# A decoder step: casts moved from GpSimd to ScalarE, a candidate key moved from PSUM to SBUF, and one wait of TensorE placed earlier

## The chip, the cores and the metric

The kernel runs on one core of a Trainium2 chip. The metric is the device time of one execution in microseconds (us). The engines are named as in the profile: PE is TensorE, DVE is VectorE, ACT is ScalarE, POOL is GpSimd, SP is SyncE, whose queue issues the transfers; PEq, ACTq, DVEq, POOLq and SPq are their sequencers. A line number such as L1545 is one of the kernel before.

## The reference

One layer of a hybrid decoder for 1024 prompt tokens and 8 decoding tokens, all in float32, model width 1024.

```python
h = modulate(rms_norm(x, ln1_g), sh1, sc1)          # sh, sc, g from silu(c) @ ada_w + ada_b
xr, gr, q, k, v, iq, ik, iw = split(h @ w_in)
xc, conv_new = causal_conv(xr, ...)                  # width 4
hr = rg_lru(xc, ...);  out_a = gelu(gr) * hr         # group A: linear recurrence
q, k = rope(rms_norm(q)), rope(rms_norm(k))          # group B: sparse attention
score = sum_h iw[h] * relu(iq[h] . ik)               # causal
idx = top_k(score, 256)                              # per query
out_b = softmax(q . k[idx]) @ v[idx]
x = x + g1 * (concat(rms_norm(out_a), rms_norm(out_b)) @ w_out)
x = x + g2 * ((silu(h2 @ w_gate) * (h2 @ w_up)) @ w_down)   # h2 from x as h above
```

## The kernel before

**Precision.** Each float32 product is made of three matmuls. An operand is split into a high part (a cast to fp32r, tiles `wH`, `cH`, `hH`) and a low part (what the cast left out, `wL`, `cL`, `hL`), and high times high, high times low and low times high are added up in PSUM. For every weight tile there is therefore a load (`wraw` or `craw`), a cast for the high part and a subtraction for the low part. The subtractions (`low`, `chunk_low`) run on POOL, the casts (`high`, `chunk_high`) mostly on ACT.

**The stage around the change** runs from about 137 to 304 us. Four things go on at once, tied by semaphores and by the order in which each engine's instructions are written.

1. *The threshold search.* For each query the 256th largest score is found by setting the bits of an integer key one after another, in `KEY_BITS` = 32 rounds. The queries are in seven groups (`NSEL`) with rows of 384 to 1025 scores. In round r, DVE counts the scores of four groups that are at least the candidate key (L1486), ACT does the other three (`signs(r)`, L973). DVE then compares the counts with a limit (L1526, L1543) and copies, under the mask `keep`, the raised candidate over the lowered one (L1545), which gives the next candidate `keyX`; both are made at the start of a round by `candidates` (L1499, an exclusive-or with a bit of `flips`). `limit`, `flips` and `raised` lie in PSUM bank 7; keys, mask and counts lie in SBUF. The copy raises `s_thr`, on which ACT's next `signs` waits.
2. *The rest of the projection.* PE computes q, k and v for nine token tiles from three weight chunks, 27 products (`NQKV`), each evacuated by ACT (`qkv_evac`) in the round that `qkv_bit` gives, 1 + n*16//26: the last in round 17. The weights of the chunk with number 3 (128x2048) are loaded when chunk 1 is used up; PE needs its low part `cL` for the last nine products.
3. *The units of the recurrent group.* Eight units of 128 weight columns (`unit`, L2238 to L2240), each 72 matmuls over all tokens, evacuated by `unit_evac` in the rounds of `UNIT_BIT`. Behind each unit PE makes the columns of the ada modulation (L2227) and the next ada product (L2221) from `adb`, a single buffer that SP loads again for each. DVE brings a row of each product to SBUF (`ada_row_late`), in fixed places of its program: behind the rounds 21, 23, 26, 28 and 31 of the search and then in the stage that follows it. Units 3 to 7 have their high parts cast by ACT in the rounds of the unit three before; the units 0 to 2 are loaded early, and POOL casts them and subtracts, once `s_thr` is at 1.
4. *POOL's row.* Behind units 0 to 2, POOL squares, scales by the gain and rotates the heads in three phases (`squared`, `rotated`, `scaled`), of which the roots are taken on DVE and ACT in rounds 8 to 10, 14 to 16 and 20 to 22. Between phase 0's rotation and its scaling stands chunk 3: a cast (L793) and the subtraction (L679). Behind phase 2's rotation come the four convolutions, with the low parts of units 3 to 7 between them. SP can issue the load of a unit and of `adb` only in the order written, behind the `wL` that frees the slot.

When the search is over, DVE turns the keys into thresholds, settles ties, and builds gates (up to about 378 us); attention, the output projection and the FFN follow. They wait for that stage.

PE asks for 24 evacuations ahead of unit 0, and for all 27 behind it:

```python
                pe.wait_ge(s_pqe, 24 if u == 0 else NQKV)
```

Of the kernel before, what the change touches and what calls it, by code (L numbers as in the profile page):

```python
# [8 lines left out]
ALU = mybir.AluOpType  # L9
# [5 lines left out]
I32 = mybir.dt.int32  # L15
# [11 lines left out]
ALLT = NTT + 1  # L27
# [32 lines left out]
NQKV = 3 * ALLT  # L60
# [14 lines left out]
SLOTS = 3  # L75
# [10 lines left out]
NSEL = len(SEL)  # L86
SEL_ACT = 4
KEY_BITS = 32

def score_banks(i, g):  # L90
    return (2 + g % 2, 3 + g % 2) if i < 4 else (2 * (g % 2), 2 * (g % 2) + 2)
# [55 lines left out]
def unit_bit(u):  # L147

    return UNIT_BIT[u]


def high_bit(u):

    return unit_bit(u - SLOTS)


def halves(w):
# [4 lines left out]
def build(nc, a, o):  # L162
    ctx = ExitStack()
    with ctx:
# [23 lines left out]
        keyC = sb("keyC", [P, NSEL], I32)  # L188
        keyXs = [sb(f"keyX{i}", [P, NSEL], I32) for i in range(2)]
        keyX = keyXs[0]  # L190
        keyM = sb("keyM", [P, NSEL], I32)
        keep = sb("keep", [P, NSEL], I32)
# [52 lines left out]
        craw = [at(f"craw{j}", [P, KD, w], C_OFF[j]) for j, (_, w) in enumerate(CHUNKS)]  # L245
        cL = [at(f"cL{j}", [P, KD, w], C_OFF[j], F32R) for j, (_, w) in enumerate(CHUNKS)]
        cH = [at(f"cH{j}", [P, KD, w], C_OFF[j] + C_LEN[j], F32R) for j, (_, w) in enumerate(CHUNKS)]
# [3 lines left out]
        wraw = [at(f"wraw{i}", [P, KD, P], RING + 4096 * i) for i in range(SLOTS)]  # L251
        wH = [at(f"wH{i}", [P, KD, P], RING + 12288 + 8192 * i, F32R) for i in range(SLOTS)]
# [76 lines left out]
        ps = ctx.enter_context(nc.psum_tensor("ps", [P, 8, 512], F32))  # L329
# [344 lines left out]
        def _(pool):  # L674
# [47 lines left out]
                pool.wait_ge(s_wH, n + (u + 1))  # L722
                pool.tensor_tensor(wL[s][:], wraw[s][:], wH[s][:].bitcast(F32), ALU.subtract).then_inc(s_wL, 1)  # L723

            pool.wait_ge(s_thr, 1)
            for u in range(SLOTS):
                pool.wait_ge(s_wr[u], 16)
                pool.tensor_copy(wH[u][:], wraw[u][:])
                pool.drain().then_inc(s_wH, 1)
                low(u)  # L730

            rope_p = consts[:, C_ROPE:C_SEL].rearrange("p (t r) -> p t r", t=ALLT)
# [55 lines left out]

            squared(0)
            rotated(0)  # L790
            pool.wait_ge(s_craw[0], 32)
            pool.wait_ge(s_pq, ALLT)
            pool.tensor_copy(cH[3][:], craw[3][:])  # L793
            pool.drain().then_inc(s_cH, 1)
            chunk_low(3)
            scaled(0)
            squared(1)
# [30 lines left out]
        def _(act):  # L828
# [22 lines left out]
                nc.scalar.copy(rows[j % 2][:], ps[:, 3 + j % 2, :]).then_inc(s_row, 1)  # L851

            def chunk_high(j):
                act.wait_ge(s_craw[j], 16)
                nc.scalar.copy(cH[j][:], craw[j][:]).then_inc(s_cH, 1)

            ada_row(0, mrow)
# [103 lines left out]
            def high(u):  # L961
                s = u % SLOTS
                act.wait_ge(s_wr[s], 16 * (u // SLOTS + 1))
                if u >= SLOTS:
                    act.wait_ge(s_un, u - SLOTS + 1)
                nc.scalar.copy(wH[s][:], wraw[s][:]).then_inc(s_wH, 1)
# [29 lines left out]
            for r in range(KEY_BITS):  # L996
                signs(r)
                for n in range(NQKV):
                    if qkv_bit(n) == r:
                        qkv_evac(n)  # L1000
                for j, (h0, h1) in enumerate(PHASE_HEADS):
                    if r == PHASE_BIT[j] + 1:
                        act.wait_ge(s_qv, j + 1)
                        A(rstd[:, :, h0:h1], rstd[:, :, h0:h1], ACT.Sqrt).then_inc(s_qr, 1)
                for u in range(NU_LRU):
                    if unit_bit(u) == r:
                        unit_evac(u)
                    if u >= SLOTS and high_bit(u) == r:
                        high(u)
            for u in range(NU_LRU):  # L1010
                if unit_bit(u) >= KEY_BITS:
                    unit_evac(u)
                    if u + SLOTS < NU_LRU:
                        high(u + SLOTS)
# [274 lines left out]
        def _(dve):  # L1289
# [199 lines left out]
            def candidates(r):  # L1489

                now, dropped = keyXs[r % 2], keyXs[(r + 1) % 2]
                m = 1 << (KEY_BITS - 1 - r)
                if r == 0:
                    V.memset(dropped[:], -0x40000001)
                    V.memset(raised, 0x40000000)
                else:
                    for n, dst in enumerate((dropped[:], raised)):
                        bit = flips[:, 2 * r - 2 + n:2 * r - 1 + n].to_broadcast([P, NSEL])
                        V.tensor_tensor(dst, now[:], bit, ALU.bitwise_xor)  # L1499

            def top_mask(key):

# [4 lines left out]

            V.memset(negb[:], NEG)
            limit, flips = ps[:, 7, 440:440 + NSEL], ps[:, 7, 448:510].bitcast(I32)
            raised = ps[:, 7, 432:432 + NSEL].bitcast(I32)  # L1510
            V.tensor_copy(limit, bounds[:])
            V.tensor_copy(flips, bits[:])
            dve.wait_ge(s_kvst, 32)
# [7 lines left out]

            for r in range(KEY_BITS):
                candidates(r)
                count(ALU.is_ge, keyXs[r % 2], 0, SEL_ACT)
                dve.drain()
                V.tensor_tensor(keep[:, 0:SEL_ACT], cnt[:, 0:SEL_ACT], limit[:, 0:SEL_ACT], ALU.is_ge)  # L1526
                for j, (h0, h1) in enumerate(PHASE_HEADS):
                    root = rstd[:, :, h0:h1]
                    if r == PHASE_BIT[j]:
                        dve.wait_ge(s_qsq, j + 1)  # L1530
                        V.tensor_reduce(root, sqh[j][:].rearrange("p t (h d) -> p t h d", d=HD), AX.X, ALU.add)
                        dve.drain()
                        V.tensor_scalar(root, root, 1.0 / HD, EPS, ALU.mult, ALU.add)
                        dve.drain().then_inc(s_qv, 1)
                    elif r == PHASE_BIT[j] + 2:
                        dve.wait_ge(s_qr, j + 1)
                        V.reciprocal(root, root)
                        dve.drain().then_inc(s_qi, 1)
                for u in range(LT + 1):
                    if unit_bit(u) + 1 == r:  # L1540
                        ada_row_late(ADA_1 + u)
                dve.wait_ge(s_sgn, r + 1)
                V.tensor_tensor(keep[:, SEL_ACT:], limit[:, SEL_ACT:], cnt[:, SEL_ACT:], ALU.is_ge)  # L1543
                dve.drain()
                V.copy_predicated(keyXs[(r + 1) % 2][:], keep[:], raised).then_inc(s_thr, 1)  # L1545
                dve.drain()
            V.tensor_scalar(keyM[:], keyX[:], 31, -2147483648, ALU.arith_shift_right, ALU.bitwise_or)
            dve.drain()
# [461 lines left out]
        def _(pe):  # L2010
# [184 lines left out]
            for n in range(NQKV):  # L2195
                j, i = 1 + n // ALLT, n % ALLT
                m = P if i < NTT else NB
                if i == 0:
                    pe.wait_ge(s_cL, j + 1)
                if n == 0:  # L2200
                    pe.wait_ge(s_re, IH * (NTT - FIRST_SEL))
                if n == 4:
                    pe.wait_ge(s_thr, 1)
                if n >= 6:
                    pe.wait_ge(s_pqe, n - 5)
                for k in range(KD):
                    act_h, act_l = hH[:, k, i * P:i * P + m], hL[:, k, i * P:i * P + m]
                    dst = ps[0:m, QKV_BANK[n % 6], 0:256]
                    mm(dst, act_h, cH[j][:, k, :], start=(k == 0), stop=False)
                    mm(dst, act_h, cL[j][:, k, :], start=False, stop=False)  # L2210
                    ins = mm(dst, act_l, cH[j][:, k, :], start=False, stop=(k == KD - 1))
                ins.then_inc(s_pq, 1)


            def ada_late(j):
# [429 lines left out]
```

## Time and profile before

| | us |
|---|---|
| median of 3 runs | 1518.95 |
| lowest and highest of the runs | 1518.07, 1521.82 |
| the profiled execution | 1521.82 |
| its span (first to last instruction) | 1520.0 |

| engine | busy us | share of the span |
|---|---|---|
| PE | 1382.2 | 91% |
| DVE | 747.7 | 49% |
| ACT | 551.4 | 36% |
| POOL | 389.2 | 26% |

The span is that of one profiled execution, 1.8 us shorter than the time of the same execution. Its engine shares are averages over very different stages, so they say little about a single one. The mean granted clock of PE was 0.944 of full speed.

### The profile page before, as it was taken

The numbers are of one execution on the slowest core, as the hardware profiler recorded it, in microseconds if no ns is written. First come the engines' busy times: TensorE is split into PE (matmuls) and PEld (weight loads), VectorE is DVE, ScalarE is ACT, GpSimd is POOL, SyncE is SP. The second block draws the span as 40 slices with busy tenths as digits, with TensorE's granted clock in tenths as the row PEclk, the third lists the DMA queues.
The fourth block names the chain that finished last, engine by engine and source line by source line (L and its number), as shares of the span: only waits on it lengthen the run. The fifth ranks groups of instructions, "written<-read, shape, count | busy, mean of one in ns | idle before, by whom it ended". The sixth has DMA issues, their size and how long they took to land.

```text
span 1520.0 us, 23593 instructions
## 1 busy us (share of the span) xinstructions
PE 1382.2 (91%) x8705; PEld 1252.8 (82%) x8705; DVE 747.7 (49%) x1642; ACT 551.4 (36%) x901; POOL 389.2 (26%) x238
## 2 busy tenths in 40 slices
PE   5889999993588988897989999999999999999998
PEld 4677998782455645897889999999999999999997
DVE  6747898599577644877601331314040413313244
ACT  5547888624766764444311111111111121111112
POOL 1222469950000001265212111121221112111210
PEclk8889999996589988999999999999999999999999
DMA  9521134430101223343111111110111111111102
GB/s 358 188 62 54 43 98 140 166 125 2 54 1 34 61 75 126 126 125 111 56 42 42 56 42 43 42 56 29 56 44 55 43 42 55 43 43 42 56 1 112
DMA packets 132226, 112.16 MB, mean 74 GB/s; under 512 B 15783, under 2 KB 116463, under 8 KB 131728
## 3 DMA queue, kind: packets, MB, share of 16 engines
q1 hardware_dynamic: 132112, 110.58, 22.7%
q8 instruction: 78, 1.28, 0.3%
q14 instruction: 36, 0.29, 0.1%
HBM read 100.74 MB, written 9.85 MB: 73 GB/s over the span
## 4 chain that ended last, share of the span: by engine, by line
PE 67%; DVE 11%; issue 6%; SPq 4%; ACT 4%; DVEq 2%; POOLq 2%; POOL 2%; DMA 1%; ACTq 1%
PE ps L2238 11%; PE ps L2240 11%; PE ps L2239 11%; PE ps L2542 5%; PE ps L2543 5%; PE ps L2544 5%; PE ps L2325 3%; PE ps L2313 2%; PE ps L2303 2%; DVE junk L1486 2%; SPq L526 1%; SPq L525 1%; PE ps L2304 1%; PE ps L2365 1%; DVE n L1293 1%
## 5 line engine op out<-in xcount | busy, mean ns | idle before, releaser
L723 POOL TENSOR_TENSOR wL<-wraw,wH 128x1024 fp32r<-128x1024 f32 x97 | 234.5, 2424 | 923.5 <-ACT wH L1227 563.9
L2238 PE MATMUL ps<-h2H,wH 128*128 128x344 f32 x1008 | 326.1, 323 | 16.9 <-issue 10.8
L2239 PE MATMUL ps<-h2L,wH 128*128 128x344 f32 x1008 | 324.9, 322 | 0.0
L2240 PE MATMUL ps<-h2H,wL 128*128 128x344 f32 x1008 | 324.8, 322 | 0.0
L1964 DVE TENSOR_TENSOR af<-ps,sg 128x1032 f32<-128x1032 f32 x22 | 27.1, 1232 | 459.3 <-PE ps L2240 451.7
L2238 PEld LDWEIGHTS ps<-h2H,wH 128*128 128x128 f32 x1008 | 192.4, 191 | 18.3 <-issue 18.3
L1293 DVE SCALAR_TENSOR_TENSOR xT<-ps,mod,xT 128x344 f32<-128x344 f32 (+3 forms) x288 | 163.0, 570 | 62.5 <-PE ps L2544 41.4
L2240 PEld LDWEIGHTS ps<-h2H,wL 128*128 128x128 f32 x1008 | 192.3, 191 | 0.0
L2239 PEld LDWEIGHTS ps<-h2L,wH 128*128 128x128 f32 x1008 | 192.3, 191 | 0.0
L2542 PE MATMUL ps<-aH,wH 128*128 128x344 f32 x480 | 153.8, 320 | 0.0
L2543 PE MATMUL ps<-aL,wH 128*128 128x344 f32 x480 | 153.4, 320 | 0.0
L2544 PE MATMUL ps<-aH,wL 128*128 128x344 f32 x480 | 153.3, 319 | 0.0
L1227 ACT CAST wH<-wraw 128x1024 fp32r<-128x1024 f32 x61 | 62.6, 1043 | 175.4 <-PE ps L2544 175.4
L973 ACT ACTIVATE junk<-score,keyX 128x896 bf16<-128x896 f32 (+2 forms) x96 | 106.0, 1106 | 19.5 <-DVE keyX L1545 13.4
L1486 DVE TENSOR_SCALAR_CACHE_REDUCE junk<-score,keyX 128x384 bf16<-128x384 f32 (+5 forms) x138 | 106.2, 826 | 0.2
L1247 ACT CAST aH<-af 128x1032 fp32r<-128x1032 f32 x22 | 23.2, 1056 | 225.9 <-DVE af L1964 225.9
L1242 ACT ACTIVATE sg<-ps 128x1032 f32<-128x1032 f32 x22 | 22.7, 1033 | 207.8 <-PE ps L2240 205.4
L2543 PEld LDWEIGHTS ps<-aL,wH 128*128 128x128 f32 x480 | 90.4, 188 | 0.0
L2544 PEld LDWEIGHTS ps<-aH,wL 128*128 128x128 f32 x480 | 90.3, 188 | 0.0
L2542 PEld LDWEIGHTS ps<-aH,wH 128*128 128x128 f32 x480 | 90.1, 188 | 0.0
L2432 PE MATMUL ps<-mixH,wH 128*128 128x384 f32 (+1 forms) x192 | 65.2, 340 | 10.1 <-DVE mixL L1780 7.4
L2238 PE MATMUL ps<-hH,wH 128*128 128x344 f32 x192 | 62.5, 326 | 1.8 <-POOL wL L723 1.8
(432 smaller groups left out, 2670.9 us busy)
## 6 DMA issues: line engine op xcount, KB each, us to landing
adb<-in_ada_w SPq DMA_DIRECT2D x8, 2048.0 KB, 8.6
wraw<-in_w_out SPq DMA_DIRECT2D x24, 512.0 KB, 3.6
wraw<-in_w_gate SPq DMA_DIRECT2D x22, 512.0 KB, 3.7
wraw<-in_w_up SPq DMA_DIRECT2D x22, 512.0 KB, 3.7
wraw<-in_w_down SPq DMA_DIRECT2D x21, 512.0 KB, 3.6
x_feature_major<-x0T SPq DMA_DIRECT2D x1, 4128.0 KB, 12.0
xin<-in_x_prompt SPq DMA_DIRECT2D x8, 512.0 KB, 7.8
ada_scale<-in_ada_w SPq DMA_DIRECT2D x2, 2048.0 KB, 12.8
```

Source lines behind the costliest of these rows:

```text
L723: pool.tensor_tensor(wL[s][:], wraw[s][:], wH[s][:].bitcast(F32), ALU.subtract).then_inc(s_wL, 1)
L973: ins = A(junk[0:m, off:off + w], score[0:m, off:off + w], ACT.Sign, scale=-1.0, bias=keyXs[r % 2][0:m, n:n + 1].bitcast(F32), accum_out=c ...
L1227: nc.scalar.copy(wH[s][:], wraw[s][:]).then_inc(s_wH, 1)
L1293: return V.scalar_tensor_tensor(out=out, in0=in0, scalar=scalar, in1=in1, op0=op0, op1=op1)
L1486: V.tensor_scalar(junk[0:m, off:off + w], score[0:m, off:off + w], thr[0:m, n:n + 1].bitcast(F32), 0.0, op, ALU.add, accum_out=cnt[0:m, n: ...
L2238: mm(dst, wH[s][:, k, :], hi[:, k, cc], start=(k == 0), stop=False)
L2239: mm(dst, wH[s][:, k, :], lo[:, k, cc], start=False, stop=False)
L2240: ins = mm(dst, wL[s][:, k, :], hi[:, k, cc], start=False, stop=(k == KD - 1))
L2432: mm(dst, wH[s][:, k, :], hi, start=(k == 0), stop=False)
L2542: mm(dst, wH[s][:, n, :], aH[:, 2 * par + f, cc], start=(f == 0), stop=False)
L2543: mm(dst, wH[s][:, n, :], aL[:, 2 * par + f, cc], start=False, stop=False)
L2544: ins = mm(dst, wL[s][:, n, :], aH[:, 2 * par + f, cc], start=False, stop=(f == 1))
```

## The change

Five edits.

- POOL no longer casts units 0 to 2; ACT does, with `high(u)` in rounds 2, 3 and 4 behind what else it has in these rounds. POOL keeps the subtractions.
- POOL no longer casts chunk 3; ACT does, with `chunk_high(3)` as the last thing of round 9.
- The raised candidate lies in the SBUF tile `keyC` in place of PSUM.
- PE waits for all 27 evacuations behind the 27 products, ahead of unit 0.
- POOL's own waits for the first threshold, the loads and the products go with the casts.

```diff
+CHUNK3_BIT = 9
...
 def high_bit(u):
-    return unit_bit(u - SLOTS)
+    return 2 + u if u < SLOTS else unit_bit(u - SLOTS)
...
-            pool.wait_ge(s_thr, 1)
             for u in range(SLOTS):
-                pool.wait_ge(s_wr[u], 16)
-                pool.tensor_copy(wH[u][:], wraw[u][:])
-                pool.drain().then_inc(s_wH, 1)
                 low(u)
...
             squared(0)
             rotated(0)
-            pool.wait_ge(s_craw[0], 32)
-            pool.wait_ge(s_pq, ALLT)
-            pool.tensor_copy(cH[3][:], craw[3][:])
-            pool.drain().then_inc(s_cH, 1)
             chunk_low(3)
...
             def chunk_high(j):
-                act.wait_ge(s_craw[j], 16)
+                act.wait_ge(s_craw[j % 3], 16 * (j // 3 + 1))
+                if j == 3:
+                    act.wait_ge(s_pq, ALLT)
                 nc.scalar.copy(cH[j][:], craw[j][:]).then_inc(s_cH, 1)
...
-                    if u >= SLOTS and high_bit(u) == r:
+                    if high_bit(u) == r:
                         high(u)
+                if r == CHUNK3_BIT:
+                    chunk_high(3)
...
-                    V.memset(raised, 0x40000000)
+                    V.memset(keyC[:], 0x40000000)
                 else:
-                    for n, dst in enumerate((dropped[:], raised)):
+                    for n, dst in enumerate((dropped, keyC)):
                         bit = flips[:, 2 * r - 2 + n:2 * r - 1 + n].to_broadcast([P, NSEL])
-                        V.tensor_tensor(dst, now[:], bit, ALU.bitwise_xor)
+                        V.tensor_tensor(dst[:], now[:], bit, ALU.bitwise_xor)
...
-            raised = ps[:, 7, 432:432 + NSEL].bitcast(I32)
...
-                V.copy_predicated(keyXs[(r + 1) % 2][:], keep[:], raised).then_inc(s_thr, 1)
+                V.copy_predicated(keyXs[(r + 1) % 2][:], keep[:], keyC[:]).then_inc(s_thr, 1)
...
                 ins.then_inc(s_pq, 1)
+            pe.wait_ge(s_pqe, NQKV)
```

## Rows read from the trace of the kernel before

**Rows 1.** Busy us (count) by stretch: PE, PEld, DVE, ACT, POOL, clock, DMA, GB/s.

```profile
137.00:304.00 167.00, 164.28 (x1213) 150.79 (x1212) 132.79 (x444) 135.72 (x264) 123.97 (x76) 0.97 0.31 102
304.00:378.00 74.00, 47.44 (x282) 38.54 (x282) 68.46 (x92) 24.52 (x30) 22.13 (x14) 0.84 0.19 64
```

**Rows 2.** The chain that ended last, 200 to 312 us: start, us, what.

```profile
216.05 4.07 POOL qk L765
...
263.18 8.81 DMA adb<-in_ada_w
...
302.02 1.90 PE ps L2221 x16
```

**Rows 3.** Timeline of ACT: start, us, line, operation, idle before and its releaser.

```profile
141.69 1.05 ACT L973 ACTIVATE junk<-score,keyX 128x896 bf16<-128x896 f32 x1 [0.49 <-DVE keyX L1545]
...
220.00 0.36 ACT L959 COPY qk<-ps 8x256 f32<-8x256 f32 x1
...
245.45 1.05 ACT L966 CAST wH<-wraw 128x1024 fp32r<-128x1024 f32 x1
246.41 1.04 ACT L973 ACTIVATE junk<-score,keyX 128x896 bf16<-128x896 f32 x1
```

**Rows 4.** Timeline of DVE, the copies under mask and one operation of round 8.

```profile
167.79 0.17 DVE L1545 COPY_PREDICATED keyX<-keep,ps 128x7 int32<-128x7 int32 x1
...
176.96 2.12 DVE L1533 TENSOR_SCALAR rstd<-rstd 128x18 f32<-128x18 f32 x1
...
196.79 0.17 DVE L1545 COPY_PREDICATED keyX<-keep,ps 128x7 int32<-128x7 int32 x1
...
200.83 0.17 DVE L1545 COPY_PREDICATED keyX<-keep,ps 128x7 int32<-128x7 int32 x1
...
216.30 0.17 DVE L1545 COPY_PREDICATED keyX<-keep,ps 128x7 int32<-128x7 int32 x1
...
318.52 0.17 DVE L1584 COPY_PREDICATED keyX<-keep,keyC 128x7 int32<-128x7 int32 x1
```

**Rows 5.** Timeline of POOL.

```profile
166.37 2.68 POOL L747 TENSOR_TENSOR qk<-qk,gqk 128x1152 f32<-128x1152 f32 x1 [0.16 <-issue]
...
174.44 4.60 POOL L679 TENSOR_TENSOR cL<-craw,cH 128x2048 fp32r<-128x2048 f32 x1 [0.18 <-POOLq L794]
...
193.15 4.03 POOL L740 TENSOR_TENSOR squares<-qk 128x2304 f32<-128x2304 f32 x1 [3.75 <-ACT qk L959]
197.34 5.18 POOL L747 TENSOR_TENSOR qk<-qk,gqk 128x2304 f32<-128x2304 f32 x1 [0.16 <-issue]
...
318.40 0.32 POOL L780 TENSOR_SCALAR gel<-stT,vec 128x8 f32<-128x8 f32 x1
...
598.52 2.35 POOL L723 TENSOR_TENSOR wL<-wraw,wH 128x1024 fp32r<-128x1024 f32 x1 [0.55 <-ACT wH L966]
```

**Rows 6.** The chain at a DVE subtraction; then its line: ns, min/median/max, first and last start.

```profile
598.89 2.40 DVE mixL L1780
...
L1780 DVE TENSOR_TENSOR mixL<-gel,mixH x12: 421/546/2453, 598.9 to 633.9; 128x384 fp32r<-128x384 f32 x8, 128x264 fp32r<-128x264 f32 x4
```

**Rows 7.** Timeline of PE.

```profile
213.78 0.32 PE L2238 MATMUL ps<-hH,wH 128*128 128x344 f32 x1
...
225.15 1.92 PE L2221 MATMUL ps<-adb,cT 128*32 128x512 f32 x16
...
272.04 3.53 PE L2221 MATMUL ps<-adb,cT 128*32 128x512 f32 x16 [1.52 <-DMA adb<-in_ada_w]
275.50 0.47 PE L2238 MATMUL ps<-hH,wH 128*128 128x344 f32 x1
...
289.68 0.42 PE L2238 MATMUL ps<-hH,wH 128*128 128x344 f32 x1
```

**Rows 8.** Timeline of DVE behind the search, the first and last of seven.

```profile
304.81 0.81 DVE L1552 TENSOR_SCALAR keyL<-keyK 128x7 int32<-128x7 int32 x1
...
325.34 1.60 DVE L1589 TENSOR_SCALAR cnt<-cnt 128x7 f32<-128x7 f32 x1
```

## The prediction, made before the change was timed

> **What bounds the kernel now.** I read first the busy time by stretch, since averages over 1520 us say nothing about an edit that touches one stage. The changed lines all run between 137 and 304 us, where the 32 rounds of the threshold search run on DVE and ACT while PE multiplies the projection. In that stretch PE is busy for 164.28 of 167 us and DVE, ACT and POOL are all between 124 and 136; behind it, up to 378, DVE works for 68.46 of 74 us and PE waits for it [rows 1]. So the question is what releases DVE at 304.
>
> The chain of waits answers it [rows 2]. From back to front: DVE's stage behind the search starts when PE's product L2221 ends at 303.9; PE is held by a transfer of `adb` that was issued at 263.18 behind POOL's work; POOL's row of operations starts at 216.05 with L765, released by round 16 of the search. So up to round 16 the search sets the end, then POOL, then PE. I call the end of PE's last product in that chain A: 302.02 + 1.90 = 303.9. Everything behind A is a chain that starts with DVE, and the change touches none of it, so I take a shift of A as the shift of the end.
>
> Third comes the timeline of ACT, to see whether it has room. In a round with nothing else in it ACT waits 0.49 us for DVE; the cast of one unit holds it for 0.96 us until its next operation (245.45 to 246.41); its last evacuation of the projection, in round 17, ends at 220.00 + 0.36 = 220.4 [rows 3].
>
> **The change part by part.**
>
> *Three casts go from POOL to ACT, in rounds 2, 3 and 4.* Each of these rounds already carries one or two evacuations on ACT, which use up the 0.49 us. So each cast lies on the path with its 0.96: +2.9 us at round 5. POOL's own time before round 5 was free: nothing waits for its units until 213.8.
>
> *The cast of chunk 3 goes to ACT, in round 9.* It has twice the columns of a unit, so I count it as two casts of 0.96. Round 9 also has evacuations and a table load, so nothing hides it: +1.9. Two things follow from its being late. PE gets chunk 3's low half, ready at 179 before and first used near 188, only at about 194, pauses about 5 us and ends the projection near 222 rather than 213.8; the evacuations of rounds 12 to 17 still find their products (only round 13 is tight, within 1 us). And POOL no longer subtracts (L679, 174.44 to 179.04) while DVE's small L1533 runs in round 8: that operation took 2.12 us and ended with POOL's [rows 4, 5], where DVE's small operations take 0.17. That gives back 1.95.
>
> *The raised candidate goes from PSUM to SBUF.* The two xors still have one operand in PSUM and write where the others write: nothing. The copy under mask (L1545) now reads mask and data from SBUF. Before, with its data in PSUM, it took 0.17 us in all of its 32 executions, also in the middle of POOL's operations: 216.30 lies inside L765 (216.05 to 220.12). A copy with both in SBUF shows only in the tail: 0.17 us at 318.52, in the middle of a POOL operation of 0.32 us (318.40) that is too short to prove much. The nearest longer case is a subtraction with both inputs in SBUF, L1780 [rows 6]: 2.40 us at 598.89 where the line's median is 0.55, beside POOL's L723 (598.52 to 600.87 [rows 5]), behind whose end it finishes within 0.5. Bounds: 0 if the copy is like the one at 318.52, the rest of the POOL operation each time if it is like L1780. I take the second, since L1780 has a long POOL operation beside it as the search will have.
>
> The Trainium skill's page "SBUF — State Buffer" (section "Who interferes with whom") says that a DVE instruction with two SBUF inputs is fully blocked by a GpSimd instruction that reads SBUF and started first. By that the sum is the one below; by the row at 318.52 it is rival one.
>
> What it costs up to round 17, placing each copy in POOL's row [rows 4, 5]. Round 6: copy at 167.79 inside L747 (to 169.05): +1.2. Round 10: chunk 3's subtraction (4.60 us) now starts with ACT's search step of round 10, whose copy would come 3.7 later: +0.9. Round 12: 196.79 inside L740 (to 197.18): +0.3. Round 13: 200.83 inside L747 (to 202.52), shifted a little: +1.0. Round 16: L765 is released by DVE itself just ahead of its copy, 216.30 against 220.12: +3.7. Together 7.1. Some 0.3 of it falls in ACT's slack.
>
> Round 17 so ends later by 2.9 + 1.9 - 1.95 + 7.1 - 0.3 = 9.6: its evacuation at 230.0 instead of 220.4.
>
> *PE waits for all 27 evacuations before unit 0.* Unit 0 started at 213.78, right behind the projection. Now it starts at 230.0. It takes 225.15 - 213.78 = 11.4 (all of PE's times here: [rows 7]). PE has been idle some 8 us then, and its clock will be at 1.2 rather than 2.4 GHz at first: behind the 1.52 us of idle ahead of 272.04, sixteen products L2221 took 3.53 us, against 1.92 at 225.15 [rows 7], which is 1.6 lost. Behind a longer gap I allow up to twice that and take 2.5. Behind unit 0 come its ada product (1.9) and five cycles of unit, columns and ada product, 14.2 each when nothing waits (275.50 to 289.68). POOL's convolution chain and its `adb` transfer, which held PE before, start from the evacuation of unit 0 and arrive about 3 us before PE wants them. So A comes at 230.0 + 11.4 + 2.5 + 1.9 + 71.0 = 316.8, against 303.9: +12.9. PE starts 16.2 later and had about 5 us of waits and slow clock on the way to A, which vanish. The copies of the later rounds are held up too, but those rounds wait for PE anyway.
>
> **The sum.** 1520.0 + 12.9 = 1532.9 of span; with the 1.8 us around it 1534.7 for the profiled execution. That one is the slowest of the three shown; against the median of 1518.95 the forecast is **1531.9**.
>
> **Rivals.**
>
> One: the copy isn't held up. Round 17 is then late by 2.9 + 1.9 - 1.95 plus about 1 for round 13's late products, 3.8; unit 0 starts at 224.2 and A comes at 311.0 by the same sum, less 0.9 for a gap of 2 to 3 us instead of 8: about +6.2, **1525**. For it: 318.52. Against it: L1780.
>
> Two: the copies meet POOL worse than placed. In round 14 or 15, for instance, a copy that comes a few tenths later than here starts inside a multiplication of 4 or 5 us instead of ahead of it. One or two such meetings are worth 3 to 7 us: +16 to +20, **1537**. It can happen since all positions shift by tenths against each other.
>
> Three, ending on the other side: the stage behind A takes up the loss. Its DVE chain holds seven operations stretched by POOL (from 304.81 to 325.34, together 7.3 us over their 0.17 [rows 8]) and 74 - 68.46 = 5.5 us of idle. If POOL's last convolution were over before DVE gets there, up to 12.8 us would come back: **1519**. The seventh is still stretched 21 us behind A, so POOL would have to be more than 20 us further ahead of A than now before all of it is back, and only all of it decides; but POOL's convolutions hang on the same unit evacuations as A, and I find them 1 to 2 us further ahead. Little speaks for it.
>
> **How the numbers follow.** The forecast has 0.66, rival one 0.2, rival two 0.08, rival three 0.04, and 0.02 is left for a gain I don't see. The forecast's own range is 1528 to 1535: 0.9 less or more for the clock (1.6 to 3.4 us lost), 2 to 3 us for the positions of the stalls. The range 1523 to 1539 takes in rival one and most of rival two. A measurement of this kernel tells about 0.3% (4.6 us) from no change. The forecast is +0.85%, rival one +0.4% and could fall short of the bound: slower 0.88, the same 0.08, faster 0.04.
>
> **What would show it.** L1545 with a minimum of 0.16 and a maximum of several us, the longest in round 16, each long one ending with a POOL operation (rival one: all 0.17). ACT's casts in rounds 2 to 4 and 9, ACT never idle in rounds 2 to 4. L1533 of round 8 at about 0.2. A gap on PE ahead of chunk 3 of about 5 us and one ahead of unit 0 of about 8, with a lower granted clock behind each. Unit 0 near 230, the last product of the chain ending near 317, and the rest of the timeline moved by the same amount. The forecast is wrong if the copy is not held up, if ACT's casts hide, or if the stage behind A is shorter than 74 us by more than 2.

## The result, and the profile after

| | before | changed |
|---|---|---|
| median, us (11 runs each) | 1518.07 | 1527.82 |
| lowest and highest | 1514.29, 1524.10 | 1525.80, 1533.62 |
| the profiled execution, its span | 1521.82, 1520.0 | 1527.64, 1525.8 |

The ratio is 1.0068, with a 95% interval of 1.0052 to 1.0085: the changed kernel is 10.3 us slower (7.9 to 12.9). Forecast were 1531.9 and +12.9; the range of 1523 to 1539 holds the time. So the direction was right, and the size is 2.6 us too large; the forecast's own, narrower range of 1528 to 1535 is missed by 0.2 us.

The line numbers are now those of the changed kernel: the copy under mask is L1542, the small operation of round 8 L1530, the cast of chunk 3 L851 and of a unit L962, its subtraction L681, the units L2236 to L2238, the ada product L2219. One thing must be known before two traces are laid side by side: in the profile of before the search begins at 141.49, in that of after at 138.05, though the code ahead of it is the same. In the eleven profiles of the experiments it begins anywhere from 137.3 to 142.1, whatever was edited. So I count from the first copy under mask of each trace, and compare A (the end of PE's last product ahead of DVE's stage) and the stage behind A in these terms.

The windows, as in [rows 1] (the stretch and its length, then the columns as there: PE, PEld, DVE, ACT, POOL, clock, DMA, GB/s):

```profile
134.00:312.50 178.50, 163.93 (x1211) 152.51 (x1210) 147.17 (x440) 140.80 (x268) 120.39 (x72) 0.96 0.29 97
312.50:386.00 73.50, 48.28 (x288) 39.39 (x290) 67.63 (x92) 24.52 (x30) 20.78 (x14) 0.83 0.19 65
188.00:195.00 7.00, 4.69 (x28) 4.69 (x29) 5.56 (x20) 6.17 (x12) 5.09 (x3) 0.76 0.00 0
226.00:232.00 6.00, 5.59 (x23) 5.59 (x24) 5.59 (x22) 5.23 (x10) 5.42 (x3) 0.60 0.00 0
232.00:240.00 8.00, 8.00 (x55) 7.79 (x58) 7.68 (x21) 5.33 (x10) 7.71 (x7) 1.00 0.00 0
```

PE's work in the search's stretch is what it was (163.93 against 164.28 us), but the stretch is some 12 us longer: PE now has gaps there. DVE is busy for 14 us more with the same work. The third row has the end of PE's first gap (ahead of chunk 3) and the fourth the start of unit 0 behind its second: the granted clock is 0.76 over 7 us and 0.60 over 6 us, and full in the fifth.

The chain of waits between the search and the units, as in [rows 2] (start, us, what):

```profile
218.64 3.85 DVE keyX L1542
222.51 1.04 ACT junk L969
...
226.00 0.37 ACT qk L955
226.41 0.66 PE ps L2236
...
310.58 1.90 PE ps L2219 x16
312.50 0.42 DVE mrowb L1516
```

Before, the chain went from round 16 to POOL, from there to the transfer of `adb`, and so to PE. Now it goes from the copy of round 16, held for 3.85 us, through ACT's counts of round 17 and its last evacuation straight to unit 0, and then PE works without a break to A at 312.5. No POOL and no transfer is left in it between 226 and 312.

### The profile page after: what moved, and what is told of

Same layout as the page of the kernel before. It is cut to its first block, busy times and chain, and to the rows that moved or that the text cites. A ratio compares the mean times of both kernels' runs of the same rounds, so it can differ in the third digit from the quotient of the medians.

```text
span 1525.8 us, 23588 instructions
## 1 busy us (share of the span) xinstructions
PE 1376.9 (90%) x8705; PEld 1251.8 (82%) x8705; DVE 760.5 (50%) x1642; ACT 556.3 (36%) x905; POOL 384.4 (25%) x234
## 4 chain that ended last, share of the span: by engine, by line
PE 69%; DVE 12%; issue 6%; ACT 5%; SPq 4%; DVEq 2%; ACTq 1%; DMA 1%; POOL 1%; POOLq 0%
PE ps L2236 12%; PE ps L2238 12%; PE ps L2237 12%; PE ps L2540 5%; PE ps L2541 5%; PE ps L2542 5%; PE ps L2323 2%; DVE junk L1484 2%; PE ps L2311 2%; PE ps L2301 2%; ACT junk L969 1%; SPq L528 1%; SPq L527 1%; PE ps L2302 1%; PE ps L2430 1%
## 5 line engine op out<-in xcount | busy, mean ns | idle before, releaser
L2236 PE MATMUL ps<-h2H,wH 128*128 128x344 f32 x1008 | 326.3, 324 | 16.3 <-issue 10.2
L2238 PE MATMUL ps<-h2H,wL 128*128 128x344 f32 x1008 | 324.8, 322 | 0.0
L2236 PEld LDWEIGHTS ps<-h2H,wH 128*128 128x128 f32 x1008 | 192.4, 191 | 17.7 <-issue 17.7
L2238 PEld LDWEIGHTS ps<-h2H,wL 128*128 128x128 f32 x1008 | 192.4, 191 | 0.0
L2236 PE MATMUL ps<-hH,wH 128*128 128x344 f32 x192 | 63.1, 328 | 9.4 <-ACT qk L955 9.1
```

The source lines that it names most:

```text
L2236: mm(dst, wH[s][:, k, :], hi[:, k, cc], start=(k == 0), stop=False)
L2238: ins = mm(dst, wL[s][:, k, :], hi[:, k, cc], start=False, stop=(k == KD - 1))
```

## The experiments

All changes of time are the ratio to the kernel before, times the median of the kernel before in the same series (1517 to 1519 us). "A" and "stage behind" are read from one profile each: A from the first copy under mask (before: 162.38), and from A to L2278, PE's first product behind A that waits for DVE (before: at 362.20, 58.33).

| kernel | time, us (95%) | A | stage behind |
|---|---|---|---|
| the change | +10.3 (7.9 to 12.9) | +12.0 | -1.4 |
| e1_copy | +7.7 (5.3 to 10.2) | +7.5 | -0.4 |
| e2_wait | +1.7 (-0.3 to 3.5) | +2.2 | -1.1 |
| e3_casts | +3.9 (2.0 to 5.8) | +4.4 | -0.4 |
| e4_psum | +3.9 (1.7 to 6.1) | +5.0 | -1.3 |
| e5_mask | +2.1 (0.3 to 4.1) | +5.1 | -1.4 |
| e6_nowait | +8.3 (5.6 to 10.9) | +9.9 | +0.2 |
| e7_units | +3.6 (1.2 to 6.2) | +4.0 | -0.9 |
| e8_chunk | -1.2 (-3.3 to 0.9) | -0.2 | +0.9 |
| e9_tail | +1.1 (-1.2 to 3.5) | -1.5 | +0.7 |
| e10_both | -3.3 (-5.3 to -1.4) | -2.3 | +0.8 |
| e11_root | -1.8 (-3.6 to 0.0) | -1.1 | -1.0 |

A and the stage together agree with the measured time within 2 us in every row. Differences below 2 us between two of these kernels are not told by the times; where I use one, it is from the traces. Nor is A exact: e9_tail is edited only behind A, and its A lies 1.5 us earlier all the same, since PE reaches unit 0 as much earlier from the first copy. The copies of the search themselves repeat to 0.02 us up to round 17 (78.72 against 78.70), so a reading of the rounds is worth more than one of A.

### The copy alone

```diff
-            raised = ps[:, 7, 432:432 + NSEL].bitcast(I32)
...
-                V.copy_predicated(keyXs[(r + 1) % 2][:], keep[:], raised).then_inc(s_thr, 1)
+                V.copy_predicated(keyXs[(r + 1) % 2][:], keep[:], keyC[:]).then_inc(s_thr, 1)
```

The kernel before with this one of the five edits (the xors and the memset go to `keyC` with it).

> The kernel before with one edit: the raised candidate lies in SBUF (keyC). Port theory (a DVE copy whose mask and data both lie in SBUF waits for the end of a running POOL operation): L1542 has a median of 0.17 us and a maximum near 4 us in round 16; round 17 ends some 8 us later, unit 0 of PE starts 2 to 3 us later, and the copies held up in rounds 18 to 31 also count since PE is not yet the only bound there: A and the median +7 to +8 us. Wait theory (the copies' delay is hidden behind PE, and the cost of the change is PE's late start alone): copies as long, but the median within +2 us, since here PE need not wait for all evacuations.

Measured 1525.92 us, +7.7. The line's summary (ns, min/median/max, then first and last start) and round 16 on DVE and on POOL:

```profile
L1544 DVE COPY_PREDICATED keyX<-keep,keyC x32: 170/223/3851, 138.0 to 300.5; 128x7 int32<-128x7 int32 x32
```

```profile
215.26 3.85 DVE L1544 COPY_PREDICATED keyX<-keep,keyC 128x7 int32<-128x7 int32 x1
```

```profile
215.02 4.07 POOL L765 TENSOR_TENSOR qk<-qk,rstd 128x2304 f32<-128x2304 f32 x1 [9.79 <-DVEq L1537]
```

POOL starts at 215.02, the copy 0.24 us later, and both end at 219.1. Round 17's copy comes 6.2 us later, less than the 8 expected. PE starts unit 0 only 0.8 us later, and not 2 to 3; the later held copies do the rest (the steps to rounds 19 and 20 are 3.3 us longer), and PE stands still for DVE's row of the ada product behind round 21:

```profile
245.53 1.87 PE L2226 MATMUL ps<-consts,mrowb 128*128 128x9 f32 x8 [9.05 <-DVEq L1519]
```

The wait theory falls: the delay is not hidden behind PE. By the medians and by the traces (A and the stage together 7.1 us, against 1.1 for the wait and 3.9 for the casts) this is the largest single term.

### PE's wait alone

```diff
                 ins.then_inc(s_pq, 1)
+            pe.wait_ge(s_pqe, NQKV)
```

> The kernel before with one edit: PE waits for all 27 evacuations before unit 0. Unit 0 starts at about 220.4 instead of 213.8 behind a gap of 6.3 us, slow clock behind it. Additive theory (PE is the bound from unit 0 to A and starts 16 us late in the changed kernel, 6.6 of it from this wait alone): +6.6 + 2 for the clock, less the 5 us of waits that PE had on its way: +3 to +4 us. Rival (the slack takes it all, since the other chain through POOL and the adb transfer sets A in the kernel before): within +1 us.

Measured 1520.55 us, +1.7: between the two, and the interval (-0.3 to 3.5) reaches into both. Unit 0 starts 6.6 us later than before, from the first copy:

```profile
216.51 0.65 PE L2239 MATMUL ps<-hH,wH 128*128 128x344 f32 x1 [6.60 <-ACT qk L959]
```

and takes 13.2 us instead of 11.4, so the ada product behind it comes 8.4 later, but A moves only by 2.2. The other 6.2 are what PE lost between that product and A in the kernel before: the 76.8 us there are 70.6 now, five cycles of 14.12. They were 1.07 us of waiting for DVE, 1.52 for `adb` at 272.04, and about 3.6 of slow clock behind the two (the granted clock is 0.81 from 239 to 243, 0.93 from 243 to 256 and 0.66 from 271 to 276). The first of them, in the kernel before (the second is in [rows 7]):

```profile
239.62 0.61 PE L2227 MATMUL ps<-consts,mrowb 128*128 128x9 f32 x4 [1.07 <-DVEq L1520]
```

### Both cast edits together

```diff
-    return unit_bit(u - SLOTS)
+    return 2 + u if u < SLOTS else unit_bit(u - SLOTS)
...
-            pool.wait_ge(s_thr, 1)
             for u in range(SLOTS):
-                pool.wait_ge(s_wr[u], 16)
-                pool.tensor_copy(wH[u][:], wraw[u][:])
-                pool.drain().then_inc(s_wH, 1)
                 low(u)
...
-            pool.tensor_copy(cH[3][:], craw[3][:])
...
+                if r == 9:
+                    chunk_high(3)
```

> The kernel before with the two cast edits (units 0 to 2 in rounds 2 to 4, chunk 3 in round 9, both on ACT), raised candidate in PSUM, no new wait of PE. L1533 of round 8 takes 0.17 us instead of 2.1. Round 17 ends 3.8 us later, PE has a gap of about 4 us ahead of chunk 3's products and starts unit 0 near 220: the median +2 to +3 us. If ACT's casts hid in its idle time, 0 or -2.

Measured 1521.32 us, +3.9, somewhat above what was expected. Round 17's copy comes 4.16 us later in the trace: the terms of the prediction, 2.9 + 1.9 - 1.95, and 1.3 more around round 13, where ACT waits 1.69 us for the product that it is to evacuate (rival one had about 1 for this).

### The changed kernel with the candidate back in PSUM

```diff
-                V.copy_predicated(keyXs[(r + 1) % 2][:], keep[:], keyC[:]).then_inc(s_thr, 1)
+                V.copy_predicated(keyXs[(r + 1) % 2][:], keep[:], raised).then_inc(s_thr, 1)
```

> The changed kernel with the raised candidate back in PSUM: casts on ACT and PE's wait stay. Port theory: all copies take 0.17 us, round 17 ends 5.8 us earlier than in the changed kernel, unit 0 starts near 224 counted on the timeline of the kernel before: +6 us against the kernel before, 6 to 7 less than the changed kernel. Wait theory (PE's wait and late chunk 3 set the time, the copies only fill the slack): +9 to +10, like the changed kernel.

Measured 1521.73 us, +3.9, somewhat less than the +6 expected, so in the changed kernel the copies are worth 10.3 - 3.9 = 6.4 us, and the rest of it 3.9. All 32 copies take 0.17 us again, and round 17's copy comes 6.5 us earlier than in the changed kernel. The rival that puts most of the loss on PE's wait falls here for the second time.

### The mask in PSUM, the candidate in SBUF

```diff
+            mask = ps[:, 7, 432:432 + NSEL].bitcast(I32)
...
-                V.tensor_tensor(keep[:, SEL_ACT:], limit[:, SEL_ACT:], cnt[:, SEL_ACT:], ALU.is_ge)
+                V.tensor_tensor(mask[:, SEL_ACT:], limit[:, SEL_ACT:], cnt[:, SEL_ACT:], ALU.is_ge)
...
-                V.copy_predicated(keyXs[(r + 1) % 2][:], keep[:], keyC[:]).then_inc(s_thr, 1)
+                V.copy_predicated(keyXs[(r + 1) % 2][:], mask, keyC[:]).then_inc(s_thr, 1)
```

The changed kernel, with the other operand moved to PSUM. It asks what about the copy matters: that its data lie in SBUF, or that both of its inputs do.

> The changed kernel with one more edit: the mask of the search's copy is written to a free corner of PSUM bank 7 instead of the SBUF tile keep. The candidate stays in the SBUF tile keyC, so the copy reads one operand from SBUF and one from PSUM. Port theory (a DVE operation is held by a running POOL operation only if both of its inputs lie in SBUF): all 32 copies take 0.17 us again and the time is that of the changed kernel with the candidate in PSUM, +3.9 us on the kernel before (2.5 to 5). Rival (the data read from SBUF is enough to hold the copy): the longest copy still takes over 3 us, and the time is that of the changed kernel, +10.3 us (8.5 to 12).

Measured 1520.75 us, +2.1, and

```profile
L1543 DVE COPY_PREDICATED keyX<-ps,keyC x32: 169/170/172, 137.3 to 296.6; 128x7 int32<-128x7 int32 x32
```

```profile
215.11 0.17 DVE L1543 COPY_PREDICATED keyX<-ps,keyC 128x7 int32<-128x7 int32 x1
```

```profile
214.85 4.06 POOL L763 TENSOR_TENSOR qk<-qk,rstd 128x2304 f32<-128x2304 f32 x1 [8.87 <-DVEq L1536]
```

The copy of round 16 meets POOL just as in the first experiment, 0.26 us into the same operation, and takes 0.17 us. One of its two inputs lies in PSUM, and it doesn't matter which. So the rival falls, and the theory stands.

### The changed kernel without PE's wait

```diff
-            pe.wait_ge(s_pqe, NQKV)
```

> The changed kernel without PE's wait for the 27 evacuations ahead of unit 0 (PE asks for 24 there, as before). Theory (the wait keeps PE idle for 8 to 9 us behind the projection, of which the lost start of unit 0 is partly used up by later waits for the search): A comes some 3 us earlier than in the changed kernel, the stage behind it is up to 1 us longer, and the time is +8 us on the kernel before (7 to 9). Rival (the later waits of PE for the search and for transfers take back all that the early start gains): +10.3 us, as the changed kernel.

Measured 1526.82 us, +8.3 against +10.3; the intervals overlap. In the trace unit 0 starts 8.4 us earlier than in the changed kernel, A comes 2.1 earlier, and the stage behind A is 1.5 longer. PE stands still at another place instead:

```profile
249.11 1.88 PE L2224 MATMUL ps<-consts,mrowb 128*128 128x9 f32 x8 [6.05 <-DVEq L1517]
```

Ahead of the columns (L2224) it waits for DVE's row of the ada product, which stands behind a round of the search. So the gap of 9.08 us that catches the eye in the changed kernel costs 2.1 us of A, and 0.5 to 2 us of time.

### The units' casts alone, and the chunk's cast alone

For the units (POOL's three casts go with it, as in the edit above):

```diff
 def high_bit(u):
-    return unit_bit(u - SLOTS)
+    return 2 + u if u < SLOTS else unit_bit(u - SLOTS)
```

> The kernel before with one edit: ACT casts units 0 to 2 in rounds 2, 3 and 4, POOL only subtracts them. Both cast edits together measured +3.9 us. Theory of the prediction (each cast lies on the search's path in full, 3 x 0.96 us): round 5 ends 2.9 us later and the time is +2.9 us (2 to 3.8). Rival (ACT's wait of 0.49 us in a round takes up half of each cast, and most of the 3.9 us belongs to chunk 3): +1.5 us or less.

Measured 1522.18 us, +3.6; round 17's copy comes 2.90 us later in the trace, three times 0.96. For the chunk:

```diff
-            pool.tensor_copy(cH[3][:], craw[3][:])
...
+                if r == 9:
+                    chunk_high(3)
```

> The kernel before with one edit: ACT casts chunk 3 in round 9, POOL only subtracts it. Theory of the prediction (+1.9 us for the cast, -1.95 us for the small DVE operation of round 8 that is no longer held): round 17 ends where it did and the time is within 1 us of before; PE has a gap of 4 to 6 us ahead of the products of chunk 3, which the search covers. Rival (PE's gap is not covered, because the products and evacuations behind it come late and the units start later): +2 us or more, with the end of A shifted by as much.

Measured 1515.97 us, -1.2, not told from nothing. Round 17's copy comes 0.11 us earlier; the step from the copy of round 9 to that of round 10 is 7.4 us instead of 5.6, the step from round 7 to round 8 5.5 instead of 7.5. Ahead of chunk 3 PE stands still for 1.37 us, not the 4 to 6 that I had expected; with both cast edits it was 5.56. Without the units' casts the chunk is there 2.7 us earlier (48.4 us from the first copy, against 51.1), and in this trace PE comes to it 1.5 later. So by these runs nearly all of what the casts cost is the units', which POOL did in time that nobody waited for.

### DVE's stage behind the search without shared inputs

[rows 8] and the copy suggest an improvement: write the small integer tiles of that stage to free corners of PSUM, so that its small operations aren't held by POOL.

```diff
+            spare = [ps[:, 7, 376 + 8 * q:376 + 8 * q + NSEL].bitcast(I32) for q in range(5)]
...
-            V.tensor_scalar(keyL[:, 0, :], keyL[:, 0, :], 1, None, ALU.add)
+            V.tensor_scalar(spare[1], spare[1], 1, None, ALU.add)
...
-            V.tensor_tensor(keyC[:], keyL[:, 1, :], keyL[:, 0, :], ALU.bitwise_or)
+            V.tensor_tensor(spare[3], spare[1], keyL[:, 1, :], ALU.bitwise_or)
```

> The kernel before; only in DVE's stage behind the search, the small integer tiles (128x7) between thresholds and ties lie in free corners of PSUM bank 7 instead of SBUF, so that no two inputs of an operation lie in SBUF and the small operations on one tile read PSUM. The last stretched operation, the subtraction on the counts (L1589 before, 1.60 us), is left as it is. Theory (these operations are stretched by POOL's running instructions in the same way as the copy was, and the stage sets the end): six of the seven stretched operations, 7.3 - 1.4 = 5.9 us, fall back to about 0.2 us each, the stage from A to PE's products of the next one is 5 to 6 us shorter, and the time is -5 us (-6 to -3). Rival (DVE waits in that stage for PE's ada rows and POOL's convolutions anyway, so that it only waits earlier): within 1.5 us of before.

Measured 1516.85 us, ratio 1.0007 (0.9992 to 1.0023): nothing. My theory fell, though its mechanism is seen. The operations are no longer held, and DVE then waits for PE:

```profile
300.24 0.17 DVE L1556 TENSOR_SCALAR ps<-ps 128x7 int32<-128x7 int32 x1
...
306.44 0.17 DVE L1503 TENSOR_SCALAR ps<-keyK 128x7 int32<-128x7 int32 x1
...
316.55 0.76 DVE L1520 COPY mrowb<-ps 128x256 f32<-128x256 f32 x2 [1.47 <-PE ps L2222]
...
330.67 0.76 DVE L1520 COPY mrowb<-ps 128x256 f32<-128x256 f32 x2 [3.42 <-PE ps L2222]
```

The second of these copies starts 31.69 us behind A; before, with all its held operations and no wait for PE, it started 31.02 behind A. PE in turn waits for POOL at the first unit behind A:

```profile
302.28 0.42 PE L2239 MATMUL ps<-hH,wH 128*128 128x344 f32 x1 [3.30 <-POOL wL L723]
```

From the first copy under mask that unit starts at 164.23, before at 164.17. So the stage behind A has two chains of nearly the same length: DVE's own, and POOL's subtractions with two units and products of PE behind them, which was 0.9 us shorter before (its product ended at A + 30.11). Without the stretched operations the second one decides. And the holds move with the work: in e9_tail a `TENSOR_SCALAR` on DVE (L1599, 128x512) that took 0.49 us before takes 2.44 at 321.50, beside POOL's L786, and ends 0.3 us behind it.

```diff
-                        V.tensor_reduce(root, sqh[j][:].rearrange("p t (h d) -> p t h d", d=HD), AX.X, ALU.add)
+                        sums = ps[:, 7, 300:300 + ALLT * (h1 - h0)].rearrange("p (t h) -> p t h", t=ALLT)
+                        V.tensor_reduce(sums, sqh[j][:].rearrange("p t (h d) -> p t h d", d=HD), AX.X, ALU.add)
...
-                        V.tensor_scalar(root, root, 1.0 / HD, EPS, ALU.mult, ALU.add)
+                        V.tensor_scalar(root, sums, 1.0 / HD, EPS, ALU.mult, ALU.add)
```

This edit on top of the one before, and alone:

> The kernel of the run before this one with one more edit: the sums of squares that DVE makes in rounds 8, 14 and 20 go to PSUM, so that the small operation on them (L1533 before, 2.12 us in round 8) reads PSUM. Theory: it takes 0.2 us in round 8, round 17 ends 2 us earlier, and PE starts the units earlier by up to that; the time is 1 to 2 us below that of the run before. Rival (PE's start of unit 0 is set by its own products, not by the search, as in the kernel before): no difference to the run before.

> The kernel before with only the sums of squares of rounds 8, 14 and 20 in PSUM. Theory: L1533 of round 8 takes 0.2 us instead of 2.12 and the time is -1 to -2 us. Rival: within 0.7 us, since PE starts unit 0 behind its own products and not behind the search.

Measured 1514.32 us, -3.3 (1.4 to 5.3 faster), for both together (2.5 below e9_tail by the medians, 0.7 by the traces), and 1515.76, -1.8, alone. The small operation of round 8 takes 0.18 us instead of 2.12, and round 17's copy comes 2.2 us earlier in both:

```profile
177.53 0.18 DVE L1534 TENSOR_SCALAR rstd<-ps 128x18 f32<-128x18 f32 x1
```

PE doesn't start the units earlier, though: its ada product behind unit 0 starts 83.6 us behind the first copy in e11_root, 83.8 in e10_both and 83.7 before. What is gone is its wait of 1.07 us for DVE. The kernel with both is faster than before (ratio 0.9978, 0.9965 to 0.9991) and some 1% faster than the changed kernel. Whether the edits behind the search add anything to that isn't told: the 1.5 us between the two kernels are less than the intervals.

## Why the prediction was right, and where its size was off

**The casts of units 0 to 2, predicted +2.9.** Right. In ACT's timeline of the changed kernel, rounds 2 to 4, the casts stand between evacuations and counts, with no idle time beside them; the step from one operation to the next is 0.95 us (147.52 to 148.47), and e7_units gave 2.90 in the trace. Below, the cast of round 2, and then the one of round 9:

```profile
147.52 1.05 ACT L962 CAST wH<-wraw 128x1024 fp32r<-128x1024 f32 x1
148.47 1.04 ACT L969 ACTIVATE junk<-score,keyX 128x896 bf16<-128x896 f32 x1
...
182.37 1.28 ACT L1000 ACT_TABLE_LOAD   x1
183.66 0.22 ACT L1000 ACTIVATE rstd<-rstd 128x18 f32<-128x18 f32 x1
183.79 1.89 ACT L851 CAST cH<-craw 128x2048 fp32r<-128x2048 f32 x1
185.58 1.03 ACT L969 ACTIVATE junk<-score,keyX 128x896 bf16<-128x896 f32 x1
```

**The cast of chunk 3, predicted +1.9, and what it gives back, 1.95.** Right. It holds ACT from 183.79 to 185.58, 1.79 us. The small operation of round 8, 2.12 us before [rows 4], is back at its own time, since POOL no longer subtracts there. In the changed kernel PE then waits 5.43 us for the chunk, where "about 5" was said, and the search covers it (a row of DVE's timeline and one of PE's):

```profile
177.47 0.18 DVE L1530 TENSOR_SCALAR rstd<-rstd 128x18 f32<-128x18 f32 x1
```

```profile
190.31 0.58 PE L2206 MATMUL ps<-cH,hH 128*128 128x256 f32 x1 [5.43 <-POOL cL L681]
```

**The copies, predicted 7.1 up to round 17, less 0.3.** Right, round by round; this is the term on which the sign hung. The line's summary in after, then the timeline of DVE in rounds 6, 10, 12, 13 and 16, and that of POOL:

```profile
L1542 DVE COPY_PREDICATED keyX<-keep,keyC x32: 170/172/3837, 138.1 to 306.5; 128x7 int32<-128x7 int32 x32
```

```profile
167.19 1.27 DVE L1542 COPY_PREDICATED keyX<-keep,keyC 128x7 int32<-128x7 int32 x1
...
189.26 1.02 DVE L1542 COPY_PREDICATED keyX<-keep,keyC 128x7 int32<-128x7 int32 x1
...
197.90 0.41 DVE L1542 COPY_PREDICATED keyX<-keep,keyC 128x7 int32<-128x7 int32 x1
...
202.03 1.61 DVE L1542 COPY_PREDICATED keyX<-keep,keyC 128x7 int32<-128x7 int32 x1
...
218.64 3.84 DVE L1542 COPY_PREDICATED keyX<-keep,keyC 128x7 int32<-128x7 int32 x1
```

```profile
165.76 2.67 POOL L745 TENSOR_TENSOR qk<-qk,gqk 128x1152 f32<-128x1152 f32 x1 [0.16 <-issue]
...
185.75 4.50 POOL L681 TENSOR_TENSOR cL<-craw,cH 128x2048 fp32r<-128x2048 f32 x1 [14.22 <-ACT cH L851]
...
194.25 4.03 POOL L738 TENSOR_TENSOR squares<-qk 128x2304 f32<-128x2304 f32 x1 [1.91 <-ACT qk L955]
198.44 5.18 POOL L745 TENSOR_TENSOR qk<-qk,gqk 128x2304 f32<-128x2304 f32 x1 [0.16 <-issue]
...
218.39 4.05 POOL L763 TENSOR_TENSOR qk<-qk,rstd 128x2304 f32<-128x2304 f32 x1 [9.82 <-DVEq L1535]
```

Each held copy ends within 0.05 us of a POOL operation. Predicted and measured over the 0.17 us of a free copy: round 6 1.2 and 1.1, round 10 0.9 and 0.9, round 12 0.3 and 0.2, round 13 1.0 and 1.4, round 16 3.7 and 3.7; together 7.1 and 7.3. Rivals one and two fall with these rows: the copies are held, and those of rounds 14 and 15 take 0.17. The Trainium skill's page "SBUF — State Buffer" (section "Who interferes with whom") has a DVE instruction with two SBUF inputs contend with a GpSimd instruction that reads SBUF. The runs agree for the copy under mask, whose mask counts as one of the two inputs: 3.85 us with both in SBUF, 0.17 with either of them in PSUM.

**Round 17, predicted 9.6 later.** It is 9.44 later (88.14 us from the first copy under mask, against 78.70).

**PE from the last evacuation to A, predicted 86.8 us (11.4 + 2.5 + 1.9 + 71.0).** Right but for 0.7. Unit 0 starts when ACT's last evacuation ends and takes 13.5 us, where 11.4 + 2.5 = 13.9 was said; the five cycles behind it take 14.12 each and not 14.2 (ACT's timeline, then PE's):

```profile
226.00 0.36 ACT L955 COPY qk<-ps 8x256 f32<-8x256 f32 x1
```

```profile
226.41 0.66 PE L2236 MATMUL ps<-hH,wH 128*128 128x344 f32 x1 [9.08 <-ACT qk L955]
...
230.59 0.44 PE L2238 MATMUL ps<-hH,wL 128*128 128x344 f32 x1
230.87 0.32 PE L2236 MATMUL ps<-hH,wH 128*128 128x344 f32 x1
```

Up to 230.8 the products follow each other every 0.29 us, from then on every 0.16: the lower and the full clock (1.2 and 2.4 GHz), after 9.08 us in which PE did nothing. About half of these 4.4 us is lost, 13.5 - 11.4 = 2.1. Altogether A is 12.0 later, where 12.9 was said; of these 0.9, 0.7 lies here and 0.2 in round 17.

**"I take a shift of A as the shift of the end."** This is the step that was off, by 1.4 us. The stage behind A is 56.94 us long instead of 58.33 (one trace each; in the kernels above whose stage isn't edited either, it differs from before by -1.4 to +0.9). It is rival three on a small scale. DVE's operations there are held less, because POOL is further ahead of A: its pair of subtractions begins 0.6 us ahead of A before and 2.1 ahead of it now (310.36 against 312.43). The seven stretched operations of before cost 7.3 us; now six cost 5.9, of which the first three and the new one, the copy under mask for three groups:

```profile
313.38 1.73 DVE L1549 TENSOR_SCALAR keyL<-keyK 128x7 int32<-128x7 int32 x1
...
315.50 1.06 DVE L1554 TENSOR_SCALAR keyN<-keyL 128x7 int32<-128x7 int32 x1
...
317.06 0.93 DVE L1559 TENSOR_SCALAR keyL<-keyL 128x7 int32<-128x7 int32 x1
...
322.92 0.93 DVE L1570 COPY_PREDICATED keyK<-keep,keyC 128x3 int32<-128x3 int32 x1
```

The same shift cut PE's wait for POOL behind A from 1.79 us to 0.35, so that both chains of the stage became shorter by the same 1.4 us (before, then changed):

```profile
305.66 0.42 PE L2238 MATMUL ps<-hH,wH 128*128 128x344 f32 x1 [1.79 <-POOL wL L723]
```

```profile
312.78 0.43 PE L2236 MATMUL ps<-hH,wH 128*128 128x344 f32 x1 [0.35 <-POOL wL L725]
```

So it isn't true that everything behind A is a chain that starts with DVE: POOL's two subtractions, begun ahead of A, release PE there. I had priced the rival at "up to 12.8, and only all of it decides", and dropped what a part of it is worth. Its top was wrong too. With PE and POOL as they are, DVE could not have had more than 0.9 us from its own side, as e9_tail shows; and even with POOL out of the way PE's two cycles behind A take 28.3 us (28.68 in the changed kernel, less the 0.35), so DVE's second row, at A + 31.02 before, could come at most some 2.7 us sooner. This last is an estimate from the two traces.

**The sum.** 12.0 - 1.4 = 10.6 us against 10.3 measured. Of the 4.1 us between 1531.9 and 1527.8, 0.9 is the median of before (1518.07 over eleven runs, not 1518.95 over three), 0.9 the search and PE up to A, 1.4 the stage behind A. The last 0.9 is within the interval of the measurement.

**The edits don't add up.** Alone they cost 7.7, 1.7 and 3.9 us, 13.3 in all, together 10.3. The interval of that difference is wider than the 3.0 us, so the times don't prove it; the traces say the same with 7.1 + 1.1 + 3.9 = 12.1 against 10.6. Part of it can be seen in the rounds: at round 17 the copy and the casts cost 6.2 and 4.2 alone and 9.4 together. The casts alone make rounds 13 and 14 1.5 us longer, by products of PE that come late; the held copies alone make them 1.2 longer, and both together also 1.2, so one delay hides the other there. Between unit 0 and A the search and PE run side by side and the later one counts; how much each edit overlaps there was not taken apart.

**What stays open.** Why the time of e5_mask came out 1.8 us below that of e4_psum, when A and the stage behind it agree within 0.2 us in their profiles; their intervals overlap.

## What to carry to other kernels

Before a small operand of a short DVE operation moves from PSUM to SBUF, lay its executions beside POOL's timeline: with all of its inputs in SBUF it may take as long as what is left of POOL's operation, and its price is the sum of these rests, not its own 0.17 us. Work on an engine that nobody waits for is free there and costs its full length on the engine that sets the pace. A gap on the bounding engine is worth what is left of it after that engine's later waits (9.08 us visible, about 2 paid), and where two chains end a stage within a microsecond of each other, shortening one of them gives at most that microsecond.

## What the runs showed of the hardware

- A copy under mask on DVE (`COPY_PREDICATED`, 128x7, int32) is held to the end of a running POOL `TENSOR_TENSOR` when mask and data both lie in SBUF: up to 3.85 us instead of 0.17 (e1_copy). With either in PSUM (before, e4_psum, e5_mask) it takes 0.17 us in all 32 executions, 0.26 us behind the start of a POOL operation of 4.06.
- A `TENSOR_SCALAR` on DVE with a single input of 128x7 in SBUF, written to SBUF, is held too: 1.73 us at 313.38, to the end of POOL's subtractions (310.36 + 4.72). L1503 took 0.96 us at 315.76 before, 0.18 behind the start of POOL's L779, a `TENSOR_SCALAR` of 2.84 us, and so was not held to the end of it; in e9_tail it writes PSUM and took 0.17 at 306.44, 0.10 behind the start of the same operation.
- PE's granted clock was lower behind both of its gaps, 0.76 from 188 to 195 us behind 5.43 us and 0.60 from 226 to 232 behind 9.08. Behind the longer one it stayed at the lower level for 4.4 us, at a price of 2.1; behind the wait of 1.52 in [rows 7] 1.6 was lost. A gap six times as long cost 0.5 us more.
